# Two norms of a two-layer block: who computes x's rows, and where the first scan keys stand

## The chip, the cores and the metric

The kernel runs on one core of a Trainium2 chip. The time is that of one execution on the device, in microseconds (us). Its engines are PE (TensorE: matmuls, with weight loads that overlap them), DVE (VectorE), ACT (ScalarE) and POOL (GpSimd). SP issues most of the loads. Each engine works through its own list of instructions in order and waits on semaphores for the others.

## The reference, cut to what matters

Two blocks of two layers each run over 256 rows of x; block 2 adds 256 rows of a context c. The change lies in block 2 alone, at the start of its layer 0 and between its two layers.

```python
for l in range(DEPTH):
    h_l = _rmsnorm(x, g_pre[l]) * (1.0 + sc_l) + sh_l      # x's rows
    h_c = _rmsnorm(xc, g_pre[l]) * (1.0 + sc_c) + sh_c     # the context's rows
    pl = _split_proj(h_l @ w_in[l])                         # queries, keys, values of the scan (GLA), ...
    pc = _split_proj(h_c @ w_in[l])
    ...
    if not last:
        xc = xc + gt_c * _rmsnorm(out_c, g_post[l])
    x = x + gt_l * _rmsnorm(out_l, g_post[l])
```

## The kernel before, in words

All matmuls are in float32, each split in three: a weight or a row is taken as a high part (rounded) and a low part (the rest), and high x high, low x high and high x low are summed. A weight unit of 128x1024 arrives by DMA in RAW; ACT copies it to its high part SPH (`split`, L1379), and DVE subtracts to get the low part SPL (L1917). There are five RAW buffers and four slots of SPH and SPL.

The rows' norm has four steps. `stats` squares and sums (one of the two tiles on ACT, one on DVE), a reciprocal root of eleven small DVE instructions follows (`rsqrt`, L1853 to L1863), and two diagonal matrices DG are made. `prod` (L970) multiplies XS by DG on PE, which turns 128 rows of it into one of eight column tiles kt in a PSUM bank. Then the tile is scaled and shifted into HV (ACT, L1418, for x; DVE, L2006, for c, whose buffer is HV_94). ACT copies HV to the high part HTH (L1421), and the low part HTL is HV minus HTH (POOL, L2519, for all of x and the odd tiles of c; DVE, L2010, for the even tiles of c). HV has two buffers, so tile kt waits until both parts of tile kt-2 are written (`mod_before`).

A planner (class `Schedule`) writes one list of steps, from which every engine takes its own in order. `take` and `give` hand out the eight PSUM banks, `get_w` names the next weight unit, and `split_upto` sets where in the lists the units are split. So the order on every engine is fixed when the program is built.

At the start of block 2's layer 0, the context's half of three scan keys (`gk_mm`, width 256) runs while x is being normed, then x's half; the other steps of the projection follow. Between the layers, the last product of layer 0 (`w2`) runs over four row tiles: x's 0 and 1, the context's 2 and 3. `x_out` squares a tile on ACT (ZB), takes its root, scales it and adds the residual (XS). Then come x's norm, four queries of x (`gq`, width 256), the context's norm ahead of the fourth query, `rank` (width 512) and four keys (`gk`, width 512), each over x and context together.

Of the kernel before, what the change touches and what calls it, by code (L numbers as in the profile page):

```python
# [5 lines left out]
F32 = mybir.dt.float32  # L6
# [29 lines left out]
EARLY = 3  # L36
# [93 lines left out]
class Schedule:  # L130
# [538 lines left out]
    def block2(self, l):  # L669
# [5 lines left out]
        self.add("wdec", l)  # L675
        early = []
        if not last:
            self.limit = self.gets + EARLY - 1
            for ft in range(EARLY):
                self.take((0, 1, 2, 3), ("gk", l, ft))  # L680
                early.append(self.get_w(f"wgk{l}", ft))
                self.add("gk_mm", l, ft, early[ft], 1)
            self.norm("x0", LOW7)
            self.add("spill_x")
            self.limit = 1 << 30
            self.split_upto(self.gets)
        self.add("mark", f"proj{l}")
        for ft, u in enumerate(early):
            self.add("gk_mm", l, ft, u, 0)
# [58 lines left out]
        for g in range(2):  # L748
            ring = ALL8 if last else (LO4, HI4)[g]
            for t in self.group_n(("w2", l, g), f"wo2{l}", g, tlist, ring, ("AB", l, "s"), g == 1, last * PF):  # L750
                if g == 1 and (last or t < 2):
                    self.x_out(l, t)
            if g == 0:
                for t in tlist:
                    self.add("x_half", l, t)
                    self.give(("w2", l, 0, t))
        if not last:
            self.add("stats", "x1")
            for t in (2, 3):
                self.split_upto(self.gets + t - 2)  # L760
                self.x_out(l, t)
# [9 lines left out]
    def x_out(self, l, t):  # L771
        self.add("x_out", l, t)
        self.give(("w2", l, 1, t))

    def run(self):
        self.ada = self.ada_te()
# [24 lines left out]
class Common:  # L801
# [27 lines left out]
    def low(self, tag, kt):  # L829

        if tag[0] in "af":
            return self.read(("prod", tag, kt))
        pool = tag[0] == "x" or kt % 2
        return self.signals["norm_pool" if pool else "norm_dve"], ("l", tag, kt)
# [49 lines left out]
def tensor_program(pe, k):  # L884
# [213 lines left out]
    def gk_mm(l, ft, u, st):  # L1098

        src = ("x1", "c1") if l else ("x0", "c0")  # L1100
        if st != 0:
# [6 lines left out]
        if not st:  # L1108
            m.then_inc(*pe.tick(mm, ("w", u), ("gk", l, ft)))
# [243 lines left out]
def scalar_program(act, k):  # L1353
# [42 lines left out]
    def stats(tag):  # L1396
        junk, _, i = norm_tiles(sb, tag)
        t = NORMS[tag][i]
        k.rows_ready(act, tag, t)
        norm_before(act, k, tag)  # L1400
        A.activation(junk[:, i, :], sb["XS"][:, t, :], ACT.Square, scale=1.0,
                     accum_out=sb["SS"][:, t:t + 1]).then_inc(*act.tick(s["norm_act"], ("sq", tag)))

    def prod(tag, kt):
# [9 lines left out]
        w = mod_tile(sb, tag)[:, kt % 2, 0:256]  # L1414
        if st == 0:
            act.wait_ge(mm, name)
# [400 lines left out]

    def x_out(l, t):
        x_square(l, 1, t)
# [23 lines left out]
def vector_program(dve, k):  # L1843
# [128 lines left out]
    def stats(tag):  # L1972
# [3 lines left out]
        x = sb["XS"][:, t, :]  # L1976
        k.rows_ready(dve, tag, t)
        norm_before(dve, k, tag)
        W.scalar_tensor_tensor(out=junk[:, i, :], in0=x, scalar=1.0, in1=x, op0=MUL, op1=MUL,
                               accum_out=sb["SS"][:, t:t + 1]).then_inc(*dve.tick(n, ("sq", tag)))  # L1980
        dve.wait_ge(s["norm_act"], ("sq", tag))
        dve.wait_ge(n, ("sq", tag))
        rsqrt(n, ("rs", tag), sb["SS"][:, 4 + t0:6 + t0], sb["SS"][:, t0:t0 + 2], 1.0 / 1024, 2)
# [6 lines left out]
    def prod(tag, kt):  # L1990
# [11 lines left out]
        o = slice(st * 256, st * 256 + 256)  # L2002
        if st:
            dve.wait_ge(mm, name)
            mod_before(dve, k, tag, kt)
            W.tensor_scalar(w, P[:, 0:256], sb["GP"][:, l, kt, st:st + 1], MT[:, l, kt, st:st + 1], MUL,  # L2006
                            ADD).then_inc(*dve.free(*k.read(name)))
            if kt % 2 == 0:
                dve.wait_ge(s["norm_act"], ("h", tag, kt))
                W.tensor_tensor(HL[:, kt, o], w, HH[:, kt, o].bitcast(F32), SUB).then_inc(  # L2010
                    *dve.tick(s["norm_dve"], ("l", tag, kt)))

# [420 lines left out]

    def x_out(l, t):
        o, x, GSS, SSO, GB = s["out_dve"], sb["XS"][:, t, :], sb["GSS"], sb["SSO"], sb["GB"]
        name = ("w2", l, 1, t)
        dve.wait_ge(s["out_act"], ("g", l, 1, t))
        W.tensor_tensor(SSO[:, 0, t:t + 1], GSS[:, 0, t:t + 1], GSS[:, 1, t:t + 1], ADD).then_inc(*dve.tick(o))
        dve.wait_ge(*dve.last)
        rsqrt(o, ("xr", l, t), SSO[:, 1, t:t + 1], SSO[:, 0, t:t + 1], 1.0 / 1024, 1)  # L2440
        dve.wait_ge(o, ("xr", l, t))
        dve.wait_ge(*k.read(("w2", l, 0, t)))
        for hf in range(2):
# [26 lines left out]
def pool_program(pool, k):  # L2470
# [403 lines left out]
```

## Time and profile before

| | us |
|---|---|
| median of 3 runs | 2202.01 |
| lowest and highest | 2199.69, 2203.01 |
| profiled execution | 2202.53 |
| its span (first to last instruction) | 2200.7 |
| PE, DVE, ACT, POOL busy | 2111.9, 1363.2, 962.2, 206.5 |

The span is what the views cover. PE is busy in 96% of it, but its busy time counts a matmul's modelled end, so the pitch from one matmul to the next is the better measure of its pace.

### The profile page before, as it was taken

How to read it: one execution, taken by the hardware profiler on the slowest of the kernel's cores; microseconds unless marked ns; L12 is line 12 of the kernel's file. 1: busy time of each engine (PE TensorE's matmuls, PEld its weight loads, DVE VectorE, ACT ScalarE, POOL GpSimd, SP SyncE). 2: the span in 40 equal slices, each digit the busy share in tenths (PEclk: the TensorE clock that was granted, in tenths of full speed). 3: DMA queues.
4: the chain of work that ended last, by engine and by line, in shares of the span. 5: the costliest groups of instructions: out<-in, count | busy, mean ns of one | idle time of the engine just before them, and what ended most of it. 6: DMA issues, size and time to landing. Idle time of an engine off the chain costs nothing.

```text
span 2200.7 us, 31532 instructions
## 1 busy us (share of the span) xinstructions
PE 2111.9 (96%) x12146; PEld 1815.8 (83%) x12146; DVE 1363.2 (62%) x2350; ACT 962.2 (44%) x1602; POOL 206.5 (9%) x173
## 2 busy tenths in 40 slices
PE   7889999989999999999999999999999999999998
PEld 5668999767999878888888778888778899888997
DVE  5635776774777524828464555878565578475565
ACT  4444555544555524345332363223234554445443
POOL 1420000041000100000010001111111000100100
PEclk9979999998999999999999999999999999999999
DMA  8434655531555432112122203534324234251543
GB/s 249 145 122 173 228 193 177 184 113 49 198 186 187 159 107 79 68 57 77 67 96 86 77 12 124 202 125 144 106 95 149 87 116 143 96 173 59 191 154 124
DMA packets 79067, 285.01 MB, mean 130 GB/s; under 512 B 8822, under 2 KB 9730, under 8 KB 78920
## 3 DMA queue, kind: packets, MB, share of 16 engines
q1 hardware_dynamic: 70560, 256.15, 34.6%
q10 hardware_dynamic: 6072, 18.73, 2.3%
q0 software_dynamic: 2288, 8.13, 1.4%
q8 instruction: 98, 1.61, 0.3%
q14 instruction: 49, 0.40, 0.1%
HBM read 277.14 MB, written 5.83 MB: 129 GB/s over the span
## 4 chain that ended last, share of the span: by engine, by line
PE 68%; DVE 8%; ACT 4%; issue 2%; POOL 0%; DVEq 0%; ACTq 0%
PE pb L924 13%; PE pb L926 13%; PE pb L925 13%; PE pb L936 5%; PE pb L938 5%; PE pb L937 5%; PE pb L942 2%; PE pb L1258 2%; PE pb L1155 2%; PE pb L1239 1%; DVE SPL L1917 1%; ACT SPH L1379 1%; PE pb L1083 1%; PE pb L1082 1%; PE pb L1081 1%
## 5 line engine op out<-in xcount | busy, mean ns | idle before, releaser
L1917 DVE TENSOR_TENSOR SPL<-RAW,SPH 128x1024 fp32r<-128x1024 f32 x433 | 524.8, 1231 | 406.2 <-ACT SPH L1379 390.5
L924 PE MATMUL pb<-HTH,SPH 128*128 128x256 f32 (+1 forms) x2008 | 649.2, 323 | 7.7 <-POOL HTL L2519 2.6
L926 PE MATMUL pb<-HTH,SPL 128*128 128x256 f32 (+1 forms) x2008 | 639.0, 318 | 0.0
L925 PE MATMUL pb<-HTL,SPH 128*128 128x256 f32 (+1 forms) x2008 | 638.9, 318 | 0.0
L1379 ACT ACTIVATE SPH<-RAW 128x1024 fp32r<-128x1024 f32 x462 | 475.6, 1049 | 269.4 <-PE pb L926 116.9
L924 PEld LDWEIGHTS pb<-HTH,SPH 128*128 128x128 f32 x2008 | 383.8, 191 | 40.3 <-issue 5.9
L925 PEld LDWEIGHTS pb<-HTL,SPH 128*128 128x128 f32 x2008 | 384.3, 191 | 26.2
L926 PEld LDWEIGHTS pb<-HTH,SPL 128*128 128x128 f32 x2008 | 383.9, 191 | 26.0
L936 PE MATMUL pb<-SPH,HTH 128*128 128x512 f32 x544 | 220.2, 405 | 16.7 <-ACT QKT L1449 6.3
L937 PE MATMUL pb<-SPH,HTL 128*128 128x512 f32 x544 | 215.6, 396 | 0.0
L938 PE MATMUL pb<-SPL,HTH 128*128 128x512 f32 x544 | 215.5, 396 | 0.0
L936 PEld LDWEIGHTS pb<-SPH,HTH 128*128 128x128 f32 x544 | 104.7, 192 | 43.6 <-issue 11.9
L924 PE MATMUL pb<-ABH,SPH 128*128 128x512 f32 (+1 forms) x384 | 131.6, 343 | 4.8 <-DVE ABL L2292 4.3
L926 PE MATMUL pb<-ABH,SPL 128*128 128x512 f32 (+1 forms) x384 | 129.8, 338 | 0.0
L925 PE MATMUL pb<-ABL,SPH 128*128 128x512 f32 (+1 forms) x384 | 129.8, 338 | 0.0
L938 PEld LDWEIGHTS pb<-SPL,HTH 128*128 128x128 f32 x544 | 104.3, 192 | 22.8
L937 PEld LDWEIGHTS pb<-SPH,HTL 128*128 128x128 f32 x544 | 104.8, 193 | 20.7
L2496 POOL TENSOR_TENSOR SPL<-RAW,SPH 128x1024 fp32r<-128x1024 f32 x29 | 69.3, 2401 | 186.1 <-ACT SPH L1379 109.3
L924 PEld LDWEIGHTS pb<-ABH,SPH 128*128 128x128 f32 x384 | 72.4, 188 | 13.6 <-ACT ABH L1790 4.7
L1740 ACT ACTIVATE GT<-pb,BG 128x512 f32<-128x512 f32 (+1 forms) x48 | 27.9, 580 | 126.7 <-PE pb L926 126.7
L926 PEld LDWEIGHTS pb<-ABH,SPL 128*128 128x128 f32 x384 | 72.2, 188 | 8.6
L925 PEld LDWEIGHTS pb<-ABL,SPH 128*128 128x128 f32 x384 | 72.3, 188 | 8.5 <-issue 0.2
(275 smaller groups left out, 2828.5 us busy)
## 6 DMA issues: line engine op xcount, KB each, us to landing
RAW<-in_w_up SPq DMA_DIRECT2D x88, 512.0 KB, 4.6
RAW<-in_wa SPq DMA_DIRECT2D x64, 512.0 KB, 3.2
RAW<-in_w_in SPq DMA_DIRECT2D x48, 512.0 KB, 4.6
RAW<-in_wmg SPq DMA_DIRECT2D x48, 512.0 KB, 3.3
RAW<-in_wbr SPq DMA_DIRECT2D x48, 512.0 KB, 3.3
RAW<-in_w_down SPq DMA_DIRECT2D x44, 512.0 KB, 4.5
RAW<-in_w_ada SPq DMA_DIRECT2D x24, 512.0 KB, 4.3
ARAW<-in_w_ada ACTq DMA_DIRECT2D x24, 512.0 KB, 4.4
```

The costliest lines, as they stand in the source:

```text
L924: T.matmul(o, wh[:, kt, :], xh[:, kt, n0:n1], start=kt == 0, stop=False)
L925: T.matmul(o, wh[:, kt, :], xl[:, kt, n0:n1], start=False, stop=False)
L926: m = T.matmul(o, wl[:, kt, :], xh[:, kt, n0:n1], start=False, stop=kt == 7)
L936: T.matmul(P[:, :], xh[:, kt, c], wh[:, j, :], start=kt == 0, stop=False)
L937: T.matmul(P[:, :], xl[:, kt, c], wh[:, j, :], start=False, stop=False)
L938: m = T.matmul(P[:, :], xh[:, kt, c], wl[:, j, :], start=False, stop=kt == 7)
L942: return T.transpose(o, i, ident)
L1155: m = T.matmul(P[:, x * 128:(x + 1) * 128], a, b, start=True, stop=True)
L1258: m = T.matmul(P[:, t * 128:(t + 1) * 128], sb["VV"][:, k0 + i, (h // 4) * 128:(h // 4 + 1) * 128], sb["APT"][:, j % 2, i * 128:(i + 1) * ...
L1379: A.activation(hi, raw, ACT.Copy, scale=1.0).then_inc(*act.tick(s["hi"], ("u", u)))
L1917: W.tensor_tensor(lo, raw, hi.bitcast(F32), SUB).then_inc(*dve.tick(s["lo_dve"], ("u", u)))
L2496: G.tensor_tensor(lo, raw, hi.bitcast(F32), SUB).then_inc(*pool.tick(s["lo_pool"], ("u", u)))
```

## The change

- At the norm of x (both layers of block 2), the odd tiles' HV is computed by DVE in place of ACT, and all of HTL by DVE in place of POOL.
- Between the layers, ACT squares the context's tiles 2 and 3 straight after their product; their two roots are taken as one, after x's norm on DVE, and the rest of `x_out` for them comes after the second and the third query.
- Two weight units are split ahead of x's norm, where three were split on ACT, and the other splits are given out one or two at a time (`ask`).
- ACT alone squares both context tiles for their norm.
- The fourth query comes before the context's norm. x's half of scan keys 0 and 1 stands ahead of that norm's products on PE and x's half of key 2 behind them; then the three context halves follow, then `rank`, then key 3 whole. This makes 72 more matmuls on PE: 144 of width 256 in place of 72 of width 512.

```diff
@@ block2
-            self.limit = self.gets + EARLY - 1
-            for ft in range(EARLY):
-                self.take((0, 1, 2, 3), ("gk", l, ft))
-                early.append(self.get_w(f"wgk{l}", ft))
-                self.add("gk_mm", l, ft, early[ft], 1)
+            self.limit = self.gets + EARLY - 1
+            self.first_keys(l, EARLY)
...
         if not last:
             self.add("stats", "x1")
             for t in (2, 3):
-                self.split_upto(self.gets + t - 2)
-                self.x_out(l, t)
-            self.split_upto(self.gets + 2)
+                self.add("x_sq", l, t)
+            self.ask(2)
             drain(self.products("x1", LOW6))
-            for ft, _ in enumerate(self.gla_queries(1, ("x1",))):
-                if ft == 0:
-                    self.add("stats", "c1")
-                if ft == 2:
-                    drain(self.products("c1", LOW6))
+            queries = self.gla_queries(1, ("x1",))
+            next(queries)
+            self.add("x_root", l, (2, 3))
+            self.ask(2)
+            next(queries)
+            self.x_out(l, 2, 2)
+            next(queries)
+            self.ask(1)
+            self.x_out(l, 3, 2)
+            drain(queries)
+            self.ask(1)
+            self.add("stats", "c1")
+            self.first_keys(1, 1)
+            self.ask(1)
+            self.first_keys(1, 1)
+            drain(self.products("c1", LOW6))
+            self.first_keys(1, 1)
             self.add("spill2")
...
+    def ask(self, n):
+        self.limit = self.splits - 1 + n
+        self.split_upto(self.limit)
+
+    def first_keys(self, l, n):
+        for ft in range(len(self.early), len(self.early) + n):
+            self.take((0, 1, 2, 3), ("gk", l, ft))
+            self.early.append(self.get_w(f"wgk{l}", ft))
+            self.add("gk_mm", l, ft, self.early[ft], 0 if l else 1)
@@ ACT prod
-        if st == 0:
+        if st == 0 and kt % 2 == 0:
             act.wait_ge(mm, name)
@@ DVE prod
-        if st:
+        if st or kt % 2:
             dve.wait_ge(mm, name)
             mod_before(dve, k, tag, kt)
             W.tensor_scalar(w, P[:, 0:256], ...)
-            if kt % 2 == 0:
-                ...
+        if st == 0 or kt % 2 == 0:
+            dve.wait_ge(s["norm_act"], ("h", tag, kt))
+            W.tensor_tensor(HL[:, kt, o], w, HH[:, kt, o].bitcast(F32), SUB)
@@ POOL prod
-        if tag[0] in "af" or tag[0] == "c" and kt % 2 == 0:
+        if tag[0] != "c" or kt % 2 == 0:
             return
```

DVE at x's norm in layer 0 had nothing between the diagonal matrices DG and a weight's low part; now it has this, and the same list stands between the layers behind two SPL:

```order
814 L2011 TENSOR_SCALAR DG_95<-IDENT,SS 128x128 x2
815 L2034 TENSOR_TENSOR HTL<-HV,HTH 128x256
816 L2030 TENSOR_SCALAR HV<-pb,GP,MODT 128x256
817 L2034 TENSOR_TENSOR HTL<-HV,HTH 128x256 x2
818 L2030 TENSOR_SCALAR HV<-pb,GP,MODT 128x256
819 L2034 TENSOR_TENSOR HTL<-HV,HTH 128x256 x2
```

The low part of tile 0 stands ahead of HV of tile 1, the low parts of tiles 1 and 2 ahead of HV of tile 3, and so on.

ACT between the layers before, from the square of x's tile (JUNK) to the start of x's norm (ZB is the square of a context tile):

```order
788 L1401 ACTIVATE JUNK,SS<-XS 128x1024
789 L1379 ACTIVATE SPH<-RAW 128x1024
790 L1812 ACTIVATE ZB,GSS<-pb 128x512
791 L1379 ACTIVATE SPH<-RAW 128x1024
792 L1812 ACTIVATE ZB,GSS<-pb 128x512
793 L1379 ACTIVATE SPH<-RAW 128x1024
794 L1418 ACTIVATE HV<-pb,MODT,GP 128x256
795 L1421 ACTIVATE HTH<-HV 128x256
796 L1418 ACTIVATE HV<-pb,MODT,GP 128x256
```

and the same place in the changed kernel:

```order
780 L1424 ACTIVATE JUNK,SS<-XS 128x1024
781 L1835 ACTIVATE ZB,GSS<-pb 128x512 x2
782 L1401 ACTIVATE SPH<-RAW 128x1024 x2
783 L1441 ACTIVATE HV<-pb,MODT,GP 128x256
784 L1444 ACTIVATE HTH<-HV 128x256 x2
785 L1441 ACTIVATE HV<-pb,MODT,GP 128x256
```

Two SPH stand between the last ZB and the first HV, where one stood; the copies to HTH come in pairs.

DVE between the layers in the changed kernel, after x's norm, from the end of the context's double root (SSO) to its norm (RS):

```order
1437 L1886 SCALAR_TENSOR_TENSOR SSO<-RS 128x2
1438 L1940 TENSOR_TENSOR SPL<-RAW,SPH 128x1024 x2
1439 L2474 SCALAR_TENSOR_TENSOR XS<-pb,SSO,GB 128x512
1440 L2476 SCALAR_TENSOR_TENSOR XS<-XS,SSO,GB 128x512
1441 L2481 TENSOR_TENSOR XS<-XS,AFX 128x1024
1442 L1940 TENSOR_TENSOR SPL<-RAW,SPH 128x1024
1443 L2474 SCALAR_TENSOR_TENSOR XS<-pb,SSO,GB 128x512
1444 L2476 SCALAR_TENSOR_TENSOR XS<-XS,SSO,GB 128x512
1445 L2481 TENSOR_TENSOR XS<-XS,AFX 128x1024
1446 L1940 TENSOR_TENSOR SPL<-RAW,SPH 128x1024
1447 L1876 TENSOR_SCALAR RS<-SS 128x2
```

Before, both context tiles' XS stood ahead of the low part of the last two queries' weights; now the weights' low parts stand between and around them.

## Rows read from the trace of the kernel before

**Rows 1.** The page, part 4: the chain that ended last, by engine

```profile
PE 68%; DVE 8%; ACT 4%; issue 2%; POOL 0%; DVEq 0%; ACTq 0%
```

**Rows 2.** Windows: start:end, length, busy PE, PEld, DVE, ACT, POOL, granted clock, DMA, GB/s

```profile
755.66:771.19 15.53, 13.70 (x107) 12.61 (x105) 2.99 (x3) 10.95 (x21) 5.84 (x8) 1.00 0.38 136
1641.56:1695.70 54.14, 50.61 (x282) 42.20 (x281) 33.74 (x68) 25.14 (x46) 11.62 (x12) 0.94 0.47 156
```

**Rows 3.** Timeline (start, length, instruction), ACT and POOL at x's norm, layer 0

```profile
756.31 0.56 ACT L1418 ACTIVATE HV<-pb,MODT,GP 128x256 f32<-128x256 f32 x1 [4.01 <-PE pb L970]
756.91 0.42 ACT L1421 ACTIVATE HTH<-HV 128x256 fp32r<-128x256 f32 x1
757.23 0.55 ACT L1418 ACTIVATE HV<-pb,MODT,GP 128x256 f32<-128x256 f32 x1
...
764.13 0.73 POOL L2519 TENSOR_TENSOR HTL<-HV,HTH 128x256 fp32r<-128x256 f32 x1 [0.18 <-ACT HTH L1421]
```

**Rows 4.** Timeline, PE there: x's last tile in key 0, and the first of rank

```profile
765.00 0.35 PE L924 MATMUL pb<-HTH,SPH 128*128 128x256 f32 x1 [0.32 <-POOL HTL L2519]
...
771.19 0.39 PE L1093 MATMUL pb<-HTH,SPH 128*32 128x512 f32 x1
```

**Rows 5.** The chain of waits between the layers: start, length, what

```profile
1652.97 1.24 POOL HTL L2519
```

**Rows 6.** Timeline, ACT between the layers, ahead of x's norm

```profile
1642.35 1.05 ACT L1379 ACTIVATE SPH<-RAW 128x1024 fp32r<-128x1024 f32 x1
1643.30 0.55 ACT L1418 ACTIVATE HV<-pb,MODT,GP 128x256 f32<-128x256 f32 x1
```

**Rows 7.** Timeline, DVE at the context's norm, tiles 0 to 4

```profile
1662.84 0.54 DVE L2006 TENSOR_SCALAR HV<-pb,GP,MODT 128x256 f32<-128x256 f32 x1
1663.86 0.43 DVE L2010 TENSOR_TENSOR HTL<-HV,HTH 128x256 fp32r<-128x256 f32 x1 [0.48 <-ACT HTH L1421]
1664.21 0.99 DVE L2006 TENSOR_SCALAR HV<-pb,GP,MODT 128x256 f32<-128x256 f32 x2
...
1666.21 0.98 DVE L2006 TENSOR_SCALAR HV<-pb,GP,MODT 128x256 f32<-128x256 f32 x2
```

**Rows 8.** Timeline, DVE: x_out of x's tile 1, the square behind it, two splits

```profile
1631.33 0.16 DVE L2438 TENSOR_TENSOR SSO<-GSS 128x1 f32<-128x1 f32 x1 [0.59 <-ACT ZB L1812]
...
1633.65 0.75 DVE L2445 SCALAR_TENSOR_TENSOR XS<-pb,SSO,GB 128x512 f32<-128x512 f32 x1
...
1636.24 1.22 DVE L1979 SCALAR_TENSOR_TENSOR JUNK<-XS 128x1024 f32<-128x1024 f32 x1
...
1655.20 2.35 DVE L1917 TENSOR_TENSOR SPL<-RAW,SPH 128x1024 fp32r<-128x1024 f32 x2
```

**Rows 9.** Timeline, PE: first of query 1, context's norm, rank, keys, values

```profile
1655.13 0.41 PE L924 MATMUL pb<-HTH,SPH 128*128 128x256 f32 x1
...
1661.90 3.73 PE L970 MATMUL pb<-DG,XS 128*128 128x128 f32 x32
...
1668.34 0.39 PE L1093 MATMUL pb<-HTH,SPH 128*32 128x512 f32 x1
...
1673.87 0.39 PE L924 MATMUL pb<-HTH,SPH 128*128 128x512 f32 x1
...
1695.63 0.39 PE L936 MATMUL pb<-SPH,HTH 128*128 128x512 f32 x1
```

**Rows 10.** Timeline, POOL: the low part of the context's last tile

```profile
1671.29 0.74 POOL L2519 TENSOR_TENSOR HTL<-HV,HTH 128x256 fp32r<-128x256 f32 x1 [1.26 <-ACT HTH L1421]
```

**Rows 11.** Windows, PE alone: length, PE busy, granted clock, DMA, GB/s

```profile
1643.90:1650.50 6.60, 4.05 (x25) 1.00 0.21 69
1650.50:1657.30 6.80, 5.82 (x23) 0.51 0.07 27
...
759.00:766.00 7.00, 5.49 (x37) 1.00 0.21 87
1596.00:1600.00 4.00, 3.98 (x11) 0.57 0.55 154
```

More of the change, by code:

```diff
@@ L675, in block2 @@
         self.add("wdec", l)
-        early = []
         if not last:
             self.limit = self.gets + EARLY - 1
-            for ft in range(EARLY):
-                self.take((0, 1, 2, 3), ("gk", l, ft))
-                early.append(self.get_w(f"wgk{l}", ft))
-                self.add("gk_mm", l, ft, early[ft], 1)
+            self.first_keys(l, EARLY)
             self.norm("x0", LOW7)
             self.add("spill_x")
-            self.limit = 1 << 30
-            self.split_upto(self.gets)
+        self.limit = 1 << 30
+        self.split_upto(self.gets)
         self.add("mark", f"proj{l}")
+        early, self.early = self.early, []
         for ft, u in enumerate(early):
-            self.add("gk_mm", l, ft, u, 0)
+            self.add("gk_mm", l, ft, u, 1 if last else 0)
             self.put_w(u)
@@ L751, in block2 @@
                 if g == 1 and (last or t < 2):
-                    self.x_out(l, t)
+                    self.add("x_sq", l, t)
+                    self.add("x_root", l, (t,))
+                    self.x_out(l, t, t)
             if g == 0:
@@ L759, in block2, with x_out @@
             for t in (2, 3):
[L760 to L762 removed]
+                self.add("x_sq", l, t)
+            self.ask(2)
             drain(self.products("x1", LOW6))
[L764 to L772 removed]
+            queries = self.gla_queries(1, ("x1",))
[15 more added lines that the diff above has]
+            self.first_keys(1, 1)
+            self.add("spill2")
+    def ask(self, n):
[6 more added lines that the diff above has]
+            self.add("gk_mm", l, ft, self.early[ft], 0 if l else 1)
+    def x_out(self, l, t, root):
+        self.add("x_out", l, t, root)
         self.give(("w2", l, 1, t))
     def run(self):
[L776 removed]
+        self.ada, self.early = self.ada_te(), []
         self.add("start")
@@ L832, in low @@
             return self.read(("prod", tag, kt))
-        pool = tag[0] == "x" or kt % 2
+        pool = tag[0] == "c" and kt % 2
         return self.signals["norm_pool" if pool else "norm_dve"], ("l", tag, kt)
@@ L1107, in gk_mm @@
             m = turned(P[:, st * 256:st * 256 + 256], *halves(u), src[st:st + 1], st * 256, st * 256 + 256)
-        if not st:
+        if st is None or st == l:
             m.then_inc(*pe.tick(mm, ("w", u), ("gk", l, ft)))
@@ L1396, in stats @@
     def stats(tag):
[L1397 to L1402, printed above, removed]
+        junk, _, on_act = norm_tiles(sb, tag)
+        for i in (0, 1) if tag == "c1" else (on_act,):
+            t = NORMS[tag][i]
+            k.rows_ready(act, tag, t)
+            norm_before(act, k, tag)
+            A.activation(junk[:, i, :], sb["XS"][:, t, :], ACT.Square, scale=1.0,
+                         accum_out=sb["SS"][:, t:t + 1]).then_inc(*act.tick(s["norm_act"], ("sq", tag)))
     def prod(tag, kt):
@@ L1816, in x_half, with x_sq @@
         x_square(l, 0, t)
-    def x_out(l, t):
+    def x_sq(l, t):
         x_square(l, 1, t)
@@ L1976, in stats @@
         x = sb["XS"][:, t, :]
-        k.rows_ready(dve, tag, t)
         norm_before(dve, k, tag)
-        W.scalar_tensor_tensor(out=junk[:, i, :], in0=x, scalar=1.0, in1=x, op0=MUL, op1=MUL,
-                               accum_out=sb["SS"][:, t:t + 1]).then_inc(*dve.tick(n, ("sq", tag)))
+        if tag != "c1":
+            k.rows_ready(dve, tag, t)
+            W.scalar_tensor_tensor(out=junk[:, i, :], in0=x, scalar=1.0, in1=x, op0=MUL, op1=MUL,
+                                   accum_out=sb["SS"][:, t:t + 1]).then_inc(*dve.tick(n, ("sq", tag)))
+            dve.wait_ge(n, ("sq", tag))
         dve.wait_ge(s["norm_act"], ("sq", tag))
-        dve.wait_ge(n, ("sq", tag))
         rsqrt(n, ("rs", tag), sb["SS"][:, 4 + t0:6 + t0], sb["SS"][:, t0:t0 + 2], 1.0 / 1024, 2)
@@ L2432, in x_half, with x_root, x_out @@
         W.tensor_copy(sb["XS"][:, t, 0:512], k.P(("w2", l, 0, t))[:, :]).then_inc(*dve.free(*k.read(("w2", l, 0, t))))
-    def x_out(l, t):
-        o, x, GSS, SSO, GB = s["out_dve"], sb["XS"][:, t, :], sb["GSS"], sb["SSO"], sb["GB"]
-        name = ("w2", l, 1, t)
[L2437 to L2441, printed above, removed]
+    def x_root(l, tl):
+        o, GSS, SSO = s["out_dve"], sb["GSS"], sb["SSO"]
+        for t in tl:
+            dve.wait_ge(s["out_act"], ("g", l, 1, t))
+        c = slice(tl[0], tl[-1] + 1)
+        W.tensor_tensor(SSO[:, 0, c], GSS[:, 0, c], GSS[:, 1, c], ADD).then_inc(*dve.tick(o))
+        dve.wait_ge(*dve.last)
+        rsqrt(o, ("xr", l, tl[0]), SSO[:, 1, c], SSO[:, 0, c], 1.0 / 1024, len(tl))
+    def x_out(l, t, root):
+        o, x, SSO, GB = s["out_dve"], sb["XS"][:, t, :], sb["SSO"], sb["GB"]
+        name = ("w2", l, 1, t)
+        dve.wait_ge(o, ("xr", l, root))
         dve.wait_ge(*k.read(("w2", l, 0, t)))
```

15 lines of the change are left out of this document (7 added, 8 removed).

## The prediction

> **What bounds the kernel now.** I read the chain of waits first: PE makes up 68% of it and DVE and ACT 12% [rows 1], so PE's own work sets the pace, and a change can gain only where PE stands still or runs at a low clock. The timeline of PE shows two such places that the change touches. At x's norm in layer 0 (place A, 755.66 to 771.19) PE has the norm's products and 72 matmuls of width 256. From 765.00 to 771.19 there are 51 of these, 0.121 us apart [rows 4], so 72 take 8.7 us. The products of a norm take 3.5 us where they run freely: between the layers, 1661.90 to 1668.34 is one norm's products and one query of 24 such matmuls, 6.44 - 2.9 [rows 9]. 15.5 - 3.5 - 8.7 leaves 3.3 us lost [rows 2]. The loss is the pace of x's rows: HV and HTH on ACT, about 1 us a tile, and POOL behind [rows 3].
>
> Between the layers (place B, 1641.56 to 1695.63) the work at full clock is 2 x 3.5 for two norms' products, 4 x 2.9 for the queries, 5.53 for rank (1668.34 to 1673.87) and 21.76 for four keys (to 1695.63) [rows 9]: 45.9 of 54.1 us. So 8.2 us are lost, nearly all before query 1 starts at 1655.13. The chain there runs through POOL's low parts of x [rows 5]. At most 8.2 + 3.3 = 11.5 us can be had.
>
> **Part 1: x's rows on two engines.** POOL leaves, and ACT loses four of eight HV. But the new lists are chains. DVE holds HTL of an even tile ahead of HV of the next odd tile, and that HTL waits for ACT's HTH; ACT holds the odd HTH, which waits for DVE's HV, ahead of the next even HV. So one pair of tiles costs: HTH to the next HV on ACT 0.32 (756.91 to 757.23), HV to HTH 0.60 (756.31 to 756.91) [rows 3], HTH 0.42 and a hand-over of 0.03, HTL to the next HV 0.35 (1663.86 to 1664.21), HV 0.54 and 0.03 [rows 3, 7]. The sum is 2.30 us a pair, against less than 2 on ACT before (from the first HV at 756.31 to POOL's last HTL at 764.13 there are 7.8 us for eight tiles). The first HTH odd starts 0.60 + 0.45 + 0.35 + 0.57 = 1.97 after the first HV, the last 3 x 2.30 later, and its HTL ends 0.45 + 0.43 after that: 9.75 us from first HV to last row.
>
> At A: 756.31 + 9.75 = 766.06, against 764.86 (764.13 + 0.73) [rows 3]. PE takes the last tile at 766.1 in place of 765.00, and the 48 matmuls of keys 1 and 2 follow as before: +1.1 us.
>
> At B: ACT has two SPH between the last ZB and HV, not one. SPH starts at 1642.35, the next 0.95 later, HV at 1644.25, against 1643.30 [rows 6]. 1644.25 + 9.75 = 1654.0. DVE has the two SPL in front, the second of which can start only after its SPH, at 1644.35 or so, and ends about 1645.8 where HTL 0 wants 1645.3; that is +0.5: 1654.5. Before, POOL's last low part ended at 1654.2 [rows 5]. So x's rows are ready 0.2 to 0.3 us later than before, and the gain that part 1 seems to bring is spent on the alternation.
>
> **Part 2: the work behind.** I count from query 1, at 1655.3. Keep the clock as before: queries 1 and 2 took 1655.13 to 1661.90 [rows 9], now they end at 1662.1. Query 3: to 1665.0. Its weights are in time: after x's last row (1654.5) DVE has the root, 2.3 us (1631.33 to 1633.65), and two SPL, 1.17 each [rows 8], to 1659.2.
> - x's half of key 0 needs its SPH, which stands behind the eviction of query 2 on ACT (0.4 after 1662.1), 1.05 us long, and the SPL of 1.2: ready at 1664.9. PE goes on: 1665.0 to 1667.9.
> - x's half of key 1 needs an SPL that stands behind XS of context tile 3 on DVE: 1664.9 + 2.6 (1633.65 to 1636.24 [rows 8]) = 1667.5, + 1.2 = 1668.7. PE waits 0.8 and is done at 1671.6.
> - The context's norm: ACT's second square starts at 1667.5 and takes 1.1; the eleven small instructions at 0.195 and the two DG take 2.6; the SPL of key 2 stands ahead of HV: 1672.5. Before, HV of the context started at 1662.84 [rows 7]: it is 9.7 us later, while only 2.9 + 2 x 2.9 us of PE's work moved ahead of it.
> - The products of that norm have four banks (0, 2, 4, 5, since keys 0, 1 and the evictions hold the others), so tile 7 waits for HV 3, which ends 3.9 after the first HV (1666.21 + 0.5 - 1662.84 [rows 7]): the products end at 1672.5 + 3.9 + 0.45 = 1676.85, 5.25 us after they started, against 3.5. That is +1.8, and x's half of key 2 stands behind them in PE's list.
> - x's half of key 2 to 1679.7. The context's last row comes 9.2 us after the first HV (1662.84 to 1672.03 [rows 7, 10]), at 1681.7; the first context half wants it at 1679.7 + 7 x 0.36 = 1682.2: just hidden. Three halves to 1688.4, rank 5.53, key 3 5.44: 1699.3 in place of 1695.63. B: +3.7 us.
>
> As a sum: later rows 0.2; three keys in halves 3 x 24 x (2 x 0.121 - 0.227) = 1.1; the wait before key 1 0.8; the products behind their banks 1.8. That is 3.9, the list above 3.7, the rest is rounding; I take 3.7. None of these has a row of its own in this order, so I bound them: at nothing if the hand-overs are faster than counted, except the 1.1, which only a gain elsewhere undoes; at twice if each link runs as under POOL's load. SP's loads of the key weights and the spills move with their steps: the spill of x and the context and the load of WDEC are issued some 9.7 us later, but rank, whose eviction waited for them before, ends 20 us later too (1693.9 in place of 1673.87 [rows 9]). From key 3 on, everything stands in the same order, so the 3.7 us are not given back.
>
> **Part 3: the clock.** In the 6.6 us before 1650.5 PE was busy 4.05 us (61%), and then the granted clock was 0.51, the level of 1.2 GHz, until 1657.3 [rows 11]. Between 1655.13 and 1657.3 that cost 1.0 us (6.77 us for 48 matmuls that take 5.8 at 0.121), 0.44 per us. At B the new stretch has the same gaps and ends at the same time, so I take the same loss; another 3.4 us at the low clock would add 1.5. At A, 759.00 to 766.00 was busy for 5.49 of 7.00 (78%) and the clock stayed at 1.00, the level of 2.4 GHz [rows 11]. Now I count for 759.1 to 766.1 two products of 0.7, five tiles in a row of 1.95 and two single ones of 0.6: 4.6 of 7 (66%), nearer to the 61% that fell. The shortest fall, 0.57 over 4 us after 1596 [rows 11], is 3.4 us at half clock (4 x 0.43/0.5), worth 3.4 x 0.44 = 1.5 us. The long one of 6.8 would cost 3.0. I take 1.5, with 0 and 3.0 as ends.
>
> The Trainium skill bears on this ("TensorE: Matmul & The Clock Gate", "HAM oscillation — how this bites in real kernels"): its rule is that only long gaps of PE bring the clock down. By it no fall comes at A, and the time would be 1.5 us less than my forecast. The trace disagrees at B: all of PE's idling in the 6.6 us before that fall sums to 2.55 us, and it was not in one piece (x's rows came a tile at a time).
>
> **The sum.** 1.1 + 1.5 at A, 3.7 at B: +6.3 on the profiled 2202.53, 2208.8. The profiled run lies 0.5 above the median of 2202.01; against the median it is 2208.3, and I say 2208. Its own range: without any fall at A and with PE's waits halved, +3; with the long falls at both places, +11: 2205 to 2213.
>
> **Rivals.**
> - *Faster: the two engines do work side by side.* If a pair took 1.35 us (ACT's HV, HTH, HTH alone: 0.32 + 0.60 + 0.42), the rows would take 1.02 + 3 x 1.35 + 0.88 = 5.95 us in place of 9.75, 3.8 less at each place. A would give 1.1 - 3.8 = -2.7 and no fall, B 3.7 - 3.8 - 1.0 for the clock = -1.1: 2198. Each 0.1 us of a pair is worth 0.8 us at both places together, so the 4.8 us of the forecast without its fall are gone at a pair of 1.7 us: that is where it decides. For it: neither engine is full at A (DVE 2.99 of 15.53 [rows 2]). Against: the order of the lists, and DVE's 0.48 us of idling before HTL in the same pattern of the context [rows 7].
> - *No change: PE's waits at B are smaller than I count.* If the key weights and the four banks cost nothing, B is +1.2 and A +1.1: 2204, and 2203 if the clock stays up at B as well. For it: my waits of 0.8 and 1.8 rest on a chain of twelve hand-overs. Against: each link is a row.
> - *Much slower: the context's rows become the bound.* They are hidden by 0.5 us only; if HV of the context comes 2 us later than I count, and the clock stays low until the third query, B is +3.7 + 1.5 + 2.8: 2213.
>
> **How the numbers follow.** Forecast 0.57, faster rival 0.15, no change 0.20, much slower 0.08. A change under 0.2% (4.4 us, so 2197.6 to 2206.4) can't be told from none. The faster rival, at 2198, falls half on either side of the lower bound: 0.08 and 0.07. The forecast's lower end (2205 to 2206.4) gives 0.10 of its 0.57 to "same". So faster 0.08, same 0.07 + 0.20 + 0.10 = 0.37, slower 0.47 + 0.08 = 0.55. The range of 8 in 10 leaves out the faster rival and half of the much slower one: 2201 to 2213.
>
> **What would show it.** In the changed profile: HTL on DVE at A with a start-to-start of 2.3 us per pair and about 0.9 us of idling for HTH in each; PE's last x tile at A about 1.1 us later; a clock under 1 after it; at B, PE's wait before the x half of key 1 put down to SPL; the products of the context's norm taking over 5 us; and the first HV of the context 31 us after PE's last product of layer 0, against 21. The prediction is wrong if x's low parts come less than 2 us a pair apart, or if PE has no gap between the queries and rank.

## The result and the profile after

The changed kernel takes 2208.22 us (median of 17 runs, 2202.59 to 2213.65), the kernel before beside it 2201.80 us (17 runs, 2197.28 to 2205.09). The ratio is 1.0033, with a 95% interval of 1.0025 to 1.0041: 6.4 us slower. The profiled execution has a span of 2206.4 us at a mean granted clock of 0.975.

The page's chain by engine, which answers to [rows 1]: PE now makes up more of it, and DVE has grown too.

```profile
PE 79%; DVE 11%; ACT 5%; issue 2%; DMA 2%; POOL 0%; DVEq 0%; ACTq 0%; SPq 0%
```

The windows of the changed kernel over both places (start:end, length, busy PE, PEld, DVE, ACT, POOL, granted clock, DMA, GB/s). They answer to [rows 2, 11]; the first two are A and B whole, from the norm's first product to the first matmul of rank (A) or of the values (B); the other three are stretches in which the clock was low.

```profile
754.86:772.96 18.10, 15.16 (x107) 14.06 (x106) 8.10 (x15) 8.77 (x17) 0.00 (x0) 0.91 0.33 117
1641.89:1701.80 59.91, 53.57 (x354) 47.72 (x353) 34.22 (x68) 26.12 (x46) 2.91 (x4) 0.91 0.39 136
764.00:768.00 4.00, 3.23 (x18) 3.05 (x19) 1.97 (x4) 2.38 (x4) 0.00 (x0) 0.76 0.78 276
1647.00:1654.00 7.00, 6.84 (x29) 6.23 (x29) 3.92 (x9) 4.07 (x10) 0.00 (x0) 0.53 0.32 113
1677.00:1681.00 4.00, 3.06 (x15) 3.07 (x16) 1.94 (x4) 1.25 (x3) 1.47 (x2) 0.57 0.16 67
```

A takes 18.10 us in place of 15.53, B 59.9 in place of 54.1. POOL has left both x norms (0.00 at A, 2.91 at B in place of 11.62), as the change says. There are three stretches at a low clock where B before had one and A none: behind A's last waits for x's rows (0.76), within x's rows at B (0.53), and behind the context's norm (0.57).

DVE and ACT at A, from the timeline of the changed kernel (start, length, instruction, idle time before it and what ended it), which answer to [rows 3]:

```profile
755.51 0.56 ACT L1441 ACTIVATE HV<-pb,MODT,GP 128x256 f32<-128x256 f32 x1 [4.02 <-PE pb L992]
756.11 0.42 ACT L1444 ACTIVATE HTH<-HV 128x256 fp32r<-128x256 f32 x1
756.89 0.54 DVE L2030 TENSOR_SCALAR HV<-pb,GP,MODT 128x256 f32<-128x256 f32 x1
757.47 0.42 ACT L1444 ACTIVATE HTH<-HV 128x256 fp32r<-128x256 f32 x1 [0.95 <-DVE HV L2030]
757.79 0.55 ACT L1441 ACTIVATE HV<-pb,MODT,GP 128x256 f32<-128x256 f32 x1
757.92 0.42 DVE L2034 TENSOR_TENSOR HTL<-HV,HTH 128x256 fp32r<-128x256 f32 x1 [0.48 <-ACT HTH L1444]
759.16 0.54 DVE L2030 TENSOR_SCALAR HV<-pb,GP,MODT 128x256 f32<-128x256 f32 x1
764.72 0.42 DVE L2034 TENSOR_TENSOR HTL<-HV,HTH 128x256 fp32r<-128x256 f32 x1 [0.48 <-ACT HTH L1444]
```

The engines take turns. Each time ACT waits 0.95 us for DVE's HV and DVE 0.48 us for ACT's HTH, and HV on DVE comes every 2.27 us (756.89, 759.16). The first row starts at 755.51, the last low part ends at 765.14: 9.63 us.

PE, same view, answering to [rows 4, 9]:

```profile
765.30 0.36 PE L946 MATMUL pb<-HTH,SPH 128*128 128x256 f32 x1 [0.77 <-DVE HTL L2034]
772.96 0.39 PE L1115 MATMUL pb<-HTH,SPH 128*32 128x512 f32 x1
...
1654.82 0.36 PE L946 MATMUL pb<-HTH,SPH 128*128 128x256 f32 x1 [0.73 <-DVE HTL L2034]
1667.91 0.35 PE L946 MATMUL pb<-HTH,SPH 128*128 128x256 f32 x1 [0.62 <-DVE SPL L1940]
1670.85 2.39 PE L992 MATMUL pb<-DG,XS 128*128 128x128 f32 x20
1673.50 1.16 PE L992 MATMUL pb<-DG,XS 128*128 128x128 f32 x8 [0.26 <-DVE HV L2030]
1675.49 0.71 PE L992 MATMUL pb<-DG,XS 128*128 128x128 f32 x4 [0.83 <-DVE HV L2030]
1677.94 0.58 PE L946 MATMUL pb<-HTH,SPH 128*128 128x256 f32 x1 [1.73 <-DVE HV L2030]
1690.81 0.39 PE L1115 MATMUL pb<-HTH,SPH 128*32 128x512 f32 x1
1701.78 0.39 PE L958 MATMUL pb<-SPH,HTH 128*128 128x512 f32 x1
```

The row at 1677.94 is the one to look at. It is x's half of key 2, whose inputs are ready, and it waits 1.73 us for an HV of the context on DVE. The half writes to a bank that one of the norm's last products holds until DVE has read it. DVE's timeline fits: the HV of tiles 5 and 6 end at 1677.88, 0.06 us before the half starts.

```profile
1676.90 0.98 DVE L2030 TENSOR_SCALAR HV<-pb,GP,MODT 128x256 f32<-128x256 f32 x2
```

### The profile page after: what moved, and what is told of

It reads as the page before. It is cut to its first block, busy times and chain, and to the rows that moved or that the text cites. A ratio compares the mean times of both kernels' runs of the same rounds, so it can differ in the third digit from the quotient of the medians.

```text
span 2206.4 us, 31643 instructions
## 1 busy us (share of the span) xinstructions
PE 2117.3 (96%) x12218; PEld 1823.6 (83%) x12218; DVE 1365.8 (62%) x2360; ACT 957.5 (43%) x1596; POOL 191.4 (9%) x157
## 4 chain that ended last, share of the span: by engine, by line
PE 79%; DVE 11%; ACT 5%; issue 2%; DMA 2%; POOL 0%; DVEq 0%; ACTq 0%; SPq 0%
PE pb L946 15%; PE pb L948 14%; PE pb L947 14%; PE pb L958 6%; PE pb L960 5%; PE pb L959 5%; PE pb L964 2%; DVE SPL L1940 2%; PE pb L1103 2%; PE pb L1105 2%; PE pb L1104 2%; PE pb L1280 2%; ACT SPH L1401 2%; PE pb L1261 1%; DMA RAW<-in_w_in 1%
## 5 line engine op out<-in xcount | busy, mean ns | idle before, releaser
L1401 ACT ACTIVATE SPH<-RAW 128x1024 fp32r<-128x1024 f32 (+1 forms) x462 | 474.9, 1048 | 278.6 <-PE pb L948 125.1
L946 PEld LDWEIGHTS pb<-HTH,SPH 128*128 128x128 f32 x2032 | 389.6, 192 | 39.1 <-issue 5.2
L947 PEld LDWEIGHTS pb<-HTL,SPH 128*128 128x128 f32 x2032 | 390.0, 192 | 25.2
L948 PEld LDWEIGHTS pb<-HTH,SPL 128*128 128x128 f32 x2032 | 389.6, 192 | 25.2
L946 PEld LDWEIGHTS pb<-ABH,SPH 128*128 128x128 f32 x384 | 72.4, 188 | 13.6 <-ACT ABH L1813 4.6
```

The lines of the kernel that those rows point to most:

```text
L946: T.matmul(o, wh[:, kt, :], xh[:, kt, n0:n1], start=kt == 0, stop=False)
L947: T.matmul(o, wh[:, kt, :], xl[:, kt, n0:n1], start=False, stop=False)
L948: m = T.matmul(o, wl[:, kt, :], xh[:, kt, n0:n1], start=False, stop=kt == 7)
L1401: A.activation(hi, raw, ACT.Copy, scale=1.0).then_inc(*act.tick(s["hi"], ("u", u)))
```

## The experiments

The stages are measured alike in every profile: A from the first product to the first rank matmul in layer 0, B from the first product to the first value matmul between the layers. The stretch from A's end to B's start is called the middle; the change touches nothing in it. A row of PE gives each end.

| kernel | A us | B us | middle us | ratio to before (95%) |
|---|---|---|---|---|
| before, first and second profile | 15.53, 15.51 | 54.07, 53.98 | 870.4, 870.2 | |
| changed, first profile | 18.10 | 59.89 | 868.9 | 1.0033 (1.0025 to 1.0041) |
| changed, second profile | 16.61 | 60.04 | 868.9 | one run |
| x's rows back | 15.49 | 57.49 | 868.8 | 1.0013 (1.0004 to 1.0022) |
| sharing alone | 16.60 | 62.51 | 869.1 | 1.0042 (1.0029 to 1.0055) |
| all banks | 16.61 | 56.19 | 868.9 | 1.0017 (1.0007 to 1.0026) |
| no halves | 18.10 | 61.68 | 870.6 | 1.0045 (1.0032 to 1.0058) |
| HV first | 13.58 | 58.82 | 869.0 | 0.9997 (0.9988 to 1.0006) |
| HV first, all banks | 13.56 | 53.70 | 868.9 | 0.9986 (0.9977 to 0.9994) |
| and one split earlier | 13.57 | 52.58 | 869.0 | 0.9979 (0.9970 to 0.9987) |
| fill | 16.61 | 60.12 | 868.9 | one run |

**x's rows back.** The changed kernel with part 1 undone: ACT makes all HV and HTH of x, POOL all low parts. The order between the layers stays.

```diff
-        pool = tag[0] == "c" and kt % 2
+        pool = tag[0] == "x" or kt % 2
... (ACT: HV of even tiles, now of all)
-        if st == 0 and kt % 2 == 0:
+        if st == 0:
... (DVE: HV and HTL of the context alone again; POOL: all HTL of x)
```

Expected: 

> The changed kernel with x's rows as they were (ACT computes every HV, POOL every HTL); the order between the layers stays changed. Place A (first product of x's norm in layer 0 to rank) took 15.5 us before and 18.1 changed, place B (the same between the layers, to the first value matmul) 54.1 and 59.9. My theory (the rows' alternation costs at A; at B the later context's rows, the banks and the low clock cost, whoever computes x's rows): A back to 15.5, B 58 to 61, the whole 2 to 3 us under the changed kernel. Rival 'the rows on two engines are the whole loss': A 15.5 and B 54 to 55, about 8 us less.

A is back at 15.49 us, so all of A's loss is part 1. B takes 57.49, half a microsecond under the range I gave: 2.4 less than in the changed kernel and 3.4 more than before, so part 2 alone costs, and the rival that has B near 54 falls. The time fell by 4.4 us (1.0033 to 1.0013 of 2201), where I forecast 2 to 3. The waits behind the queries are the same to 0.07 us. In this execution the clock stayed up all through B (start:end, length, PE busy, granted clock, DMA, GB/s, and the wait in PE's timeline):

```profile
1637.48:1644.00 6.52, 4.54 (x34) 1.00 0.35 95
1641.00:1700.00 59.00, 52.87 (x355) 1.00 0.42 142
```

```profile
1662.29 0.35 PE L946 MATMUL pb<-HTH,SPH 128*128 128x256 f32 x1 [0.61 <-DVE SPL L1940]
1672.39 0.39 PE L946 MATMUL pb<-HTH,SPH 128*128 128x256 f32 x1 [1.73 <-DVE HV L2030]
```

The two waits of 0.6 and 1.7 us belong to part 2, whoever makes x's rows. The 2.4 us that B gains have two sources. From key 2's half to rank there are 11.61 us (1672.39 to 1684.00) in place of 12.87, since no fall of the clock came: 1.3. And query 1 starts 12.17 us after the first product (1649.65 - 1637.48) in place of 13.36: 1.2. So part 1 costs at B as well. In the kernel before, POOL made its first four low parts of x beside DVE's work on the context, and they took 5.23 us:

```profile
1644.38 5.23 POOL L2519 TENSOR_TENSOR HTL<-HV,HTH 128x256 fp32r<-128x256 f32 x4 [47.62 <-ACT HTH L1421]
```

In the new order that work comes later, POOL's low parts take 0.72 to 0.74 us each behind the first two (1.79 us together), and the last ends 11.6 us after the first product (1649.08 - 1637.48), against 12.65 before and 12.77 in the changed kernel. The new order alone brings x's rows 1.05 us earlier; part 1 loses this again.

**Sharing alone.** The reverse: the kernel before with part 1 and nothing else.

```diff
-        pool = tag[0] == "x" or kt % 2
+        pool = tag[0] == "c" and kt % 2
... (ACT: HV of even tiles alone)
... (DVE: HV also of x's odd tiles, and all HTL of x; POOL: none of x)
-        if st:
+        if st or kt % 2:
```

Expected: 

> The kernel before with only the sharing of x's rows between ACT and DVE; the order of the steps between the layers stays as it was, so each of DVE's shares of x's rows stands behind both of its finishings of x (1.1 us root and 1.2 us of adding each) and its low halves of weights. Theory: layer 0 as the changed kernel, 16.6 us at full clock and 18.1 us with the fall of the clock; between the layers x's last row comes 2 to 5 us later than before and the stage takes 57 to 62 us (before 54.1); whole 5 to 10 us over before. Rival (DVE has room there, and the order does not matter): 54 to 55 us between the layers, whole 1 to 3 us over before.

A is 16.60 us, and the whole is 9.2 us slower (1.0042 of 2200), as the theory says. B is 62.5, half a microsecond over the range I gave, and x's last low part comes 7.6 us later than before, not 2 to 5. I had looked at the sum of DVE's work and not at its first share. PE's timeline, then DVE's:

```profile
1651.80 1.22 PE L970 MATMUL pb<-DG,XS 128*128 128x128 f32 x4 [8.72 <-DVE HV L2006]
```

```profile
1642.56 1.22 DVE L2452 TENSOR_TENSOR XS<-XS,AFX 128x1024 f32<-128x1024 f32 x1
1643.70 1.22 DVE L1917 TENSOR_TENSOR SPL<-RAW,SPH 128x1024 fp32r<-128x1024 f32 x1
1644.84 0.15 DVE L2438 TENSOR_TENSOR SSO<-GSS 128x1 f32<-128x1 f32 x1
...
1648.60 1.22 DVE L2452 TENSOR_TENSOR XS<-XS,AFX 128x1024 f32<-128x1024 f32 x1
1649.74 1.22 DVE L1917 TENSOR_TENSOR SPL<-RAW,SPH 128x1024 fp32r<-128x1024 f32 x1
1650.87 0.42 DVE L2010 TENSOR_TENSOR HTL<-HV,HTH 128x256 fp32r<-128x256 f32 x1
1651.21 0.54 DVE L2006 TENSOR_SCALAR HV<-pb,GP,MODT 128x256 f32<-128x256 f32 x1
```

HV of x's tile 1 stands behind the finishing of two context tiles, so PE has no bank for 8.72 us, and the granted clock is at 0.50 from 1648 to 1664. The reordering of part 2 is what makes part 1 bearable at B: it moves x's rows ahead of that work.

**All banks.** The changed kernel, where the context's products may use all eight banks.

```diff
-            drain(self.products("c1", LOW6))
+            drain(self.products("c1", ALL8))
```

Expected: 

> The changed kernel with all eight banks open to the products of the context's norm in place of six. Theory (products wait for HV because of four free banks, and key 2 then takes a bank that tile 6 of them still holds): the products take 3.5 to 4 us in place of 5.1, the 1.7 us wait ahead of x's half of key 2 goes, no low clock there, PE then waits for the context's last row at most 1 us: B 56 to 57 in place of 59.9, A unchanged, the whole -3 to -4. Rival 'the context's rows are the bound, the banks only show it': the waits come back ahead of the context halves, B stays at 59 to 60.

B is 56.19 us, as forecast, 3.7 less than in the changed kernel. The waits of 0.26 and 0.83 us within the norm are gone, and that before key 2's half is 0.92 where it was 1.73:

```profile
1665.81 0.36 PE L946 MATMUL pb<-HTH,SPH 128*128 128x256 f32 x1 [0.61 <-DVE SPL L1940]
1673.40 0.39 PE L946 MATMUL pb<-HTH,SPH 128*128 128x256 f32 x1 [0.92 <-DVE HV L2030]
```

From key 1's half to key 2's there are 7.59 us, in the changed kernel 10.03 (1667.91 to 1677.94): 2.4 us of the 3.7 are these waits. The other 1.3 are the clock. From key 2's half to rank there are four halves of 24 matmuls, 11.6 us at 0.121; the changed kernel needs 12.87 (1677.94 to 1690.81), and this one had no low clock there. By the two ratios (1.0033 and 1.0017) the whole is 3.5 us shorter; their intervals just overlap, so the stage is the firmer evidence.

**No halves.** The changed kernel without the three x halves between the layers; the keys run at full width behind rank, as before.

```diff
             self.add("stats", "c1")
-            self.first_keys(1, 1)
             self.ask(1)
-            self.first_keys(1, 1)
             drain(self.products("c1", LOW6))
-            self.first_keys(1, 1)
```

Expected: 

> The changed kernel without the three early x halves of the scan keys between the layers: all four keys are computed whole behind rank, as before; x's rows and the order of x_out stay changed. Theory (the halves cover the context's norm; without them PE stands still from the queries to the context's rows, about 9 us of work missing): PE idles 5 to 9 us between query 3 and rank with the clock falling, B 61 to 66, the whole +2 to +6 over the changed kernel. Rival 'the halves are the cost (more matmuls, a bank held)': B 55 to 57, the whole -3 to -5.

B is 61.68 us, in the range. PE stands still for 6.08 us before the context's products:

```profile
1670.73 5.45 PE L989 MATMUL pb<-DG,XS 128*128 128x128 f32 x26 [6.08 <-DVE DG L2008]
```

In the new order the halves are worth 1.8 us in the profile (2.6 by the two ratios). They are the cover for a norm that the reordering makes late, not a gain over the kernel before, where PE had no such gap.

**HV first.** The changed kernel, where DVE takes HV of x's odd tile ahead of the low part of the even one.

```diff
-        if st == 0 or kt % 2 == 0:
-            dve.wait_ge(s["norm_act"], ("h", tag, kt))
-            W.tensor_tensor(HL[:, kt, o], w, ...)
+        for j in (kt,) if st and kt % 2 == 0 else (kt - 1, kt) if st == 0 and kt % 2 else ():
+            dve.wait_ge(s["norm_act"], ("h", tag, j))
+            W.tensor_tensor(HL[:, j, o], mod_tile(sb, tag)[:, j % 2, 0:256], ...)
```

Expected: 

> The changed kernel with DVE's list at x's norm turned round: HV of an odd tile stands ahead of HTL of the even tile before it; same engines, same instructions. Theory (the 2.27 us per pair come from the order of the two lists): a pair takes 1.3 to 1.5 us, x's last row comes 3 to 3.8 us earlier at each place, A 18.1 to 13.0-14.0 with the clock at 1.00, B 59.9 to 55-57, the whole -8 us. Rival 'DVE and ACT hinder one another, or PSUM reads do': a pair stays above 2 us and nothing moves by more than 1 us.

A is 13.58 us, within the theory's 13.0 to 14.0: 4.5 less than the changed kernel's first profile, 3.0 less than its second, 1.9 less than before. The whole is 7.9 us under the changed kernel by the two ratios, as forecast. A pair of tiles takes 1.55 us, a little more than the 1.3 to 1.5 of the theory, as DVE's HV at B show:

```profile
1639.25 0.54 DVE L2030 TENSOR_SCALAR HV<-pb,GP,MODT 128x256 f32<-128x256 f32 x1
...
1640.80 0.54 DVE L2030 TENSOR_SCALAR HV<-pb,GP,MODT 128x256 f32<-128x256 f32 x1
```

B missed: 58.82 where I forecast 55 to 57. x's rows come earlier there too, but DVE's late HV of the context still hold key 2's bank, and the clock falls behind that wait (PE's timeline, then its windows):

```profile
1668.64 0.58 PE L946 MATMUL pb<-HTH,SPH 128*128 128x256 f32 x1 [1.73 <-DVE HV L2030]
```

```profile
1660.00:1666.00 6.00, 5.11 (x43) 1.00 0.45 160
1666.00:1674.00 8.00, 6.07 (x29) 0.62 0.37 153
```

The fall is a long one here: from key 2's half to rank there are 14.26 us (1668.64 to 1682.90) for what takes 11.6 at the high clock, 2.7 us in place of the changed kernel's 1.3. The wait and this fall are why B missed.

**HV first, all banks.** Both edits.

Expected: 

> The changed kernel with two edits: for x's rows DVE takes the product of the odd tile before the low half of the even one, and the context's last eight products may use all eight banks. My theory (in this stage the end is set by the pair of tiles on ACT and DVE, and behind the queries by banks that products hold while DVE is late): first product to first rank matmul in layer 0 takes 13.6 us as in the run with the first edit alone (changed kernel 18.1, before 15.5); between the layers both waits behind the products go, among them the 1.7 us before key 2's x half, and with it the fall of the clock behind it, so first product to first value matmul takes 51 to 53 us (first edit alone 58.8, second alone 56.2, before 54.1). Whole: 3 to 5 us under the kernel before. Rival (the clock gives the gain back, as it did with the first edit alone): 55 to 57 us between the layers, whole equal to the kernel before or up to 1 us under it.

B is 53.70 us, 0.7 over the theory's range and below the rival's. The wait before key 2's half is 0.90, and the clock falls once, early in x's rows, not behind the context's norm. The kernel is faster than before: 2197.32 us (11 runs) against 2200.12 (23 runs), 0.9977 to 0.9994, or 3.1 us by the ratio, at the lower end of the theory's 3 to 5. So these two faults turned a gain into a loss. No run opens the banks with x's rows left on ACT and POOL, so how much of the gain at B part 2 would bring without part 1 is open.

**And one split earlier.** As the last, with one of two weight splits ahead of ACT's square (ZB) of row tile 3, which is the context's; the expectation calls it x's.

```diff
-            for t in (2, 3):
-                self.add("x_sq", l, t)
-            self.ask(2)
+            self.add("x_sq", l, 2)
+            self.ask(1)
+            self.add("x_sq", l, 3)
+            self.ask(1)
```

Expected: 

> As e5_hv_banks, and one of the two weight splits that stand on ACT between its square of x's tile 3 and the first row of x is put ahead of that square, where ACT stood idle for 3.5 us in the run with the first edit alone. Theory: x's rows begin 1.0 us earlier and nothing else moves, so the stage between the layers takes 1 us less than e5_hv_banks, 50 to 52 us. Rival (DVE's low halves of the two weights, 2.36 us for both, or PE's products set the start of x's rows): no difference to e5_hv_banks within 0.3 us.

ACT in this kernel; the stage's first product is at 1638.79.

```profile
1635.36 1.05 ACT L1402 ACTIVATE SPH<-RAW 128x1024 fp32r<-128x1024 f32 x1
1638.99 0.60 ACT L1836 ACTIVATE ZB<-pb 128x512 f32<-128x512 f32 x1 [2.58 <-PE pb L961]
1639.57 1.05 ACT L1402 ACTIVATE SPH<-RAW 128x1024 fp32r<-128x1024 f32 x1
1640.52 0.56 ACT L1442 ACTIVATE HV<-pb,MODT,GP 128x256 f32<-128x256 f32 x1
```

The first HV comes 1.73 us after the first product (2.67 without the edit: 1642.76 - 1640.09), and B is 52.58, 1.1 less; the difference is as forecast, the range of 50 to 52 was missed by 0.6. 0.94 of that is the earlier start; the clock, which stayed up all through B here, can have given the rest. It takes 2196.21 us (12 runs), ratio 0.9970 to 0.9987: 4.6 us under the kernel before, the best of all. Its advantage over the last one, 1.1 us, is within the spread of the two sets of runs; the stage shows it, the ratio alone does not.

**Both kernels once more, and fill.** The remaining question was the clock. The kernel before and the changed kernel were profiled again; and in a third profile nine matmuls whose result nobody reads were put into PE's waits at A of the changed kernel.

Expected of the kernel before: 

> The kernel before, profiled once more. Of its span, 870.4 us lay between the first rank matmul of layer 0 and the first product between the layers; in the seven profiles of changed kernels it was 868.8 to 869.0 us five times, 869.1 in the one that is built on the kernel before, and 870.6 once. Theory (chance of the single execution): 868.7 to 869.1 us here, a span of 2198 to 2201 us, and the two stages as before, 15.5 and 54.1 us. Rival (the kernel before is slower there, and the change gains 1.5 us in the part it does not touch): 870 us again.

Expected of the changed kernel: 

> The changed kernel, profiled once more. Between the layers 59.5 to 60.2 us from the first product to the first value matmul, with the 1.7 us wait before key 2's x half. In layer 0 the fall of the clock behind PE's waits of 0.3 to 0.8 us came in two of four profiles with these waits (18.1 us), and not in the two others (16.6 us). Theory (chance of the single execution): either of the two, 18.1 or 16.6 us. Rival (the fall belongs to this kernel): 18.1 us.

Expected of fill: 

> The changed kernel with three more matmuls of 256 columns, into a bank that nobody reads, ahead of each of tiles 5, 6 and 7 in key 0's x half in layer 0, where PE waits for x's rows. Theory: at full clock the nine matmuls (1.1 us at 0.12 us each) fit into the waits of 0.3 to 0.8 us, so the first rank matmul comes 16.5 to 17.0 us after the first product and the clock stays at 1.00; if the fall of the clock behind these waits is what took 1.5 us of the 18.1 in the changed kernel, filling them removes it. Rival (the fall has nothing to do with these waits): the clock falls at the same place and the stage takes 18.1 to 19.0 us.

```diff
+                    if kt >= 5:
+                        for _ in range(3):
+                            T.matmul(k.banks[7][:, 0:256], wh[:, kt - 1, :], HH[:, kt - 1, 0:256], ...)
```

The changed kernel's second profile has the same waits at A to 0.01 us, and no fall behind them (PE's windows):

```profile
764.00:768.00 4.00, 4.00 (x36) 1.00 0.93 287
768.00:772.00 4.00, 4.00 (x24) 1.00 0.67 228
```

B is 60.04 us, within the forecast. Of five profiles with these waits at A the clock fell in two (changed kernel's first, no halves: 18.10 us), and stayed up in three (changed kernel's second, sharing alone, all banks: 16.6). Fill gave 16.61 with the clock up, but so did three of five without it: it shows that the nine matmuls fit into the waits, and settles nothing on the cause.

The kernel before gave 870.2 us for the middle again, so my forecast of 868.7 to 869.1 missed. The 1.4 us go with a fall of the clock behind a wait near 1596, in the second profile of the kernel before:

```profile
1596.00:1600.00 4.00, 4.00 (x13) 0.66 0.67 209
```

and in the changed kernel's first and second profile the same window reads

```profile
1596.00:1600.00 4.00, 3.05 (x12) 1.00 0.11 18
```

```profile
1596.00:1600.00 4.00, 4.00 (x19) 1.00 0.97 389
```

I had that fall in [rows 11], as a yardstick for the shortest fall. It came in both profiles of the kernel before and in one of the ten of all other kernels (no halves, middle 870.6). Those three have a middle of 870.2 to 870.6 us, the nine without it 868.8 to 869.1. The waits ahead of it are the same in the kernel before and the changed one (1.54 and 0.76 us), and nothing in the middle was edited. Whether the shift of work ahead of it decides, or chance, is open.

## Why the prediction was right

The forecast was 2208 us and the time is 2208.22. The mechanisms held except for the clock in x's rows at B, one term was too small, and what I had missed on either side nearly cancelled.

- **A pair of x's tiles, 2.30 us, 9.75 in all.** It is 2.27 and 9.63. The neighbours' rows were enough, because both links occur in the trace before.
- **A, +1.1 us.** 16.61 against 15.51 in the second profiles: 1.10.
- **A, +1.5 us for the clock.** The size was right (18.10 - 16.60 = 1.50), the certainty not: it came in two of five profiles. On average it is worth 0.6 us.
- **B, x's rows 0.2 to 0.3 us later.** The last low part ends 12.77 us after the first product (1654.66 - 1641.89), before 12.65: 0.1. But this is a difference of two effects, as "x's rows back" shows: the new order brings the rows 1.05 us earlier and part 1 makes them 1.2 later. I had seen that a gain is spent on the alternation, not where it comes from.
- **B, the same loss by the clock in x's rows.** It was not the same. The fall came earlier (0.53 over 1647 to 1654), while PE waited for rows anyway, and was over when query 1 began; before, the low level reached into the queries and cost 1.0 us. That is a gain of 1.0, with the 0.1 above in it: query 1 starts 13.36 us after the first product in place of 13.57, and the three queries take 8.94 us (1655.25 to 1664.19) in place of 9.73. By the Trainium skill ("TensorE: Matmul & The Clock Gate", "HAM oscillation — how this bites in real kernels") only long gaps bring the clock down; the longest here ahead of the fall is 1.13 us, so the trace disagrees after the change as before it.
- **B, 0.8 us before key 1's half, for its SPL.** The row says 0.62 us idle, but that is counted from a matmul's modelled end; from key 0's half to key 1's there are 3.72 us (1664.19 to 1667.91), 0.8 more than its 24 matmuls take.
- **B, 1.1 us for the narrow matmuls.** The pitches bear it out: a half takes 2.9 us (four in 11.6, "all banks"), a whole key 5.45 (1696.33 to 1701.78), and 3 x (5.8 - 5.45) is 1.1. No run had full-width keys in that place with the rest alike.
- **B, the context's products 5.25 us long behind four banks.** From 1670.85 to 1676.20 (1675.49 + 0.71) there are 5.35.
- **B, key 2's half directly behind them.** Here the term was mis-sized: 1.8 us for the banks, and from the norm's first product to key 2's half there are 7.09 us (1670.85 to 1677.94) where the kernel before has 3.48 from the norm's first product to the query behind it: 3.6. The half waits 1.73 us, for a bank that the planner gave to a product of tile 6 and that DVE reads late. I counted the banks for the products and not for the step behind them. The low clock after it adds 1.3 us (12.87 - 11.6). "All banks" shows both.
- **B, the context's last row just hidden.** POOL's last low part ends at 1680.68, and no context half waits for one.
- **B as a whole, +3.7.** 5.8 in the first profiles: -1.0 (x's rows and queries) + 0.8 (SPL) + 1.1 (narrow matmuls) + 3.6 (banks) + 1.3 (low clock) = 5.8, each from the start of one step to the start of the next. In the second profiles it is 6.1.
- **The first HV of the context.** It starts 29.7 us after the end of layer 0's last product (1671.55 - 1641.89), where I had said 31 (before 21): the 1.0 us that the clock did not cost makes up most of this.
- **Not in the sum:** the middle, -1.4 us, which goes with the clock at 1596.

The sum of what the runs show is 1.1 + 0.6 + 5.9 (the mean of 5.8 and 6.1) - 1.4 = 6.2 us, measured 6.4. So the closeness of 2208 is partly luck: B was 2.2 us too small, and A's fall of the clock (0.9 too large on average) and the middle (1.4) made up for it.

The rivals: "faster" named the right condition, a pair under 1.7 us. With 1.55 us in "HV first" A gains as it says (13.6 against 15.5), and the whole comes to no measurable difference, since B's bank wait stayed. "No change" fell with the two waits at B, both there. "Much slower" needed the context's rows to bound, and they stayed hidden.

## What to carry to other kernels

When two engines share the tiles of a chain, the order within each list can set the pace, and not the load: put what the other engine waits for ahead of what only finishes one's own tile. Here that exchange on DVE turned 2.27 us a pair into 1.55. Before work is moved off an engine, ask what slowed it there: POOL's low parts at B were slow beside DVE's work, which the new order moved away in any case. When work is moved ahead of a norm or another consumer, follow the banks of the step *behind* the products too, and compare the stage's length between profiles before explaining a difference of whole times of a few microseconds.

## What was not expected of the hardware

With waits that are equal to 0.01 us, TensorE's clock fell in some executions of one and the same program and not in others: at A, behind waits of 0.31 to 0.78 us, from 2.4 to 1.2 GHz in one of two profiles of the changed kernel, for 1.5 us of loss, and among programs with these same waits in "no halves" but not in "sharing alone" and "all banks"; at B, behind the wait of 1.73 us, in the changed kernel (both profiles), fill and "HV first", at a price of 1.3 to 2.7 us, but not in "x's rows back". Of the 17 executions of the changed kernel, the two fastest (2202.6 and 2202.7 us) are the two with the highest mean granted clock, 0.981 against 0.975 to 0.979. What decides between a fall and none is open. So a fall read from one profile is a possibility with a price, and its chance needs several profiles.
